# Expert stage of a routed encoder layer: token rows fetched in four column pieces and turned by VectorE

## The chip, the cores and the metric

The kernel runs on one core of one Trainium2 chip. The metric is device time in microseconds (us) of one execution. A core has five instruction queues that matter here: TensorE (PE, matmuls; PEld is its weight load, which overlaps), VectorE (DVE), ScalarE (ACT), GpSimd (POOL) and SyncE (SP). SP issues the plain DMAs, POOL the indirect ones (rows picked by an index) and some small ones. All transfers of a core run on its 16 DMA engines. Data lies in SBUF as 128 partitions; matmul results go to PSUM.

## The reference, cut to what matters

One layer of a streaming encoder over 2048 prompt rows and 128 sample rows of 1024 values, all float32. Token mixing and cross-attention come first and are not touched by the change beyond the places where the expert stage overlaps their end. The expert stage sends every row to 2 of 32 SwiGLU experts:

```
lg = t @ w_rg + b_rg ;  g_idx = argmax(lg) ;  g_w = softmax(lg)[g_idx]
le = (t @ w_re + b_re)[group g_idx] ;  top_v, top_i = top_k(le, 2)
gate = g_w * softmax(top_v) ;  expert = g_idx * 8 + top_i
y = (silu(x @ w_eg[e]) * (x @ w_eu[e])) @ w_ed[e]     # w_eg, w_eu: 1024 x 512, w_ed: 512 x 1024
x = x + sum over the two experts of gate * y ;  out = rms_norm(x) * g_final
```

The experts' sum over the 1024 input values may be taken in any order, as long as the rows of the weights are taken in the same one.

## The kernel before, in words

**Lists.** The attention stage (functions `scores`, `residual`, `logits`, `route`, `place`) ends with each row's two experts. POOL scatters one entry per row and expert into a table in DRAM (`scatter_slots`). One step of the expert stage computes 128 entries: 64 of an expert below 16 (lane 0) and 64 of one from 16 up (lane 1), since PE's output halves can hold two experts side by side. There are steps 0 to 41. Step 0 is computed between the last parts of the attention stage (`gate_early`, `up_early`, `down_early`), steps 1 to 41 by `work`, written out for the first and last ones and looped in between.

**What one step does, engine by engine.**

- POOL, in this order in `work(t)`: `gather_x` fetches the 128 residual rows of step t into `r_x`; `gather(t + 2)` fetches the 128 normalised input rows of step t+2 into `r_x1n`, with the row numbers in `e_token`; `fetch(t + 3)` and `fetch_again(t + 1)` load the lists `e_pair` and `e_spair` in two pieces each; `scatter_x` writes the finished rows back to DRAM; `scatter_out` writes the final output rows. `gather_x(t + 1)` waits for the landing of `scatter_x(t)`, since a row can occur in both. That loop of scatter, landing, gather, landing and addition must close once a step.
- PE, in `work(t)`: gate product (8 k-slices, each two matmuls of 64 stationary columns that run side by side, one for each lane, helper `both`), up product in two halves, `turn_h` of the first half of the hidden rows (2 transposes), `turn_x(t + 1)` (8 transposes of the next step's input rows, L2195, into `r_pst`), `turn_h` of the second half, down product (16 pairs into `r_psx`). Within the down product the order was: k-slices 0 and 1 for both output halves, then 2 and 3.
- ACT: `silu`, then one copy of 256 columns of the turned hidden rows (L1775, needed by the down product's first pairs), then the copy of the first four turned k-slices of the input, `r_pst` to `r_h2T` (L1780), then sums of squares.
- DVE: `tokens(t + 2)` (one cast of the row list, L1957), `rows`, two products of the hidden halves (L1974), the copy of the second half of the turned hidden rows (L1979), the copy of the second four k-slices of the turned input (L1962), two additions of the expert's result (L1993), and the final scaling (L2002).
- SP: loads of the next expert's weights, 2 MB each for gate, up and down, when PE has finished with the buffer (`load_part`, L1286).

Semaphores alone tie the queues; each engine takes its own instructions strictly in order. Several names are reused buffers: `r_x1n` holds the gathered input rows, `r_h2T` their transposes (two buffers each), `r_x1r` holds the SiLU output, the hidden rows and their transposes, and `W` the weights.

**Entry.** Before step 1, PE waits for the rows of step 1: DVE writes the step table, POOL fetches the list (L1584), DVE casts it (L1957), POOL gathers the rows (L1600), PE turns them (L2195), ACT and DVE copy them, and the gate product starts. DVE has the cast for step 2 ahead of its copy for step 1, and that cast waits for step 2's list, which POOL fetches behind step 1's gather.

## Time and profile before

| | us |
|---|---|
| median of 3 runs | 2452.66 (2451.31 to 2457.74) |
| the profiled execution's own time | 2455.3 |
| its span | 2453.6 |
| PE busy | 2385.9 (97%) |
| DVE busy | 1015.2 (41%) |
| ACT busy | 448.8 (18%) |
| POOL busy | 560.1 (23%) |

The span runs from the first to the last recorded instruction; the execution's time is 1.7 us longer. Busy time counts each engine by itself, and a matmul's recorded length (0.59 us for 512 columns) overlaps the next one's, so the distance between starts (0.43 us for a pair) says how fast PE goes. Gate steps of the expert stage follow each other every 22.25 us. In a timeline row the first number is the start, the second the length, and the bracket at the end says how long the engine had been idle and what ended that.

### The profile page before, as it was taken

To read this page: it belongs to the slowest core of one execution; us is meant where nothing else is said; L and a number is where in the kernel's file an instruction comes from. 1 tells how busy PE (TensorE), PEld (TensorE's weight loads), DVE (VectorE), ACT (ScalarE), POOL (GpSimd) and SP (SyncE) were. 2 spreads that over 40 slices of the span, in tenths; PEclk is the share of its full clock that TensorE was granted. 3 is DMA by queue.
4 is the path that set the end of the run, shared out by engine and by line. 5 is a ranking of instruction groups with operands and counts; after the bars stand their busy time and mean duration, and the time that the engine had idled before them with its cause. 6 is when DMAs were issued, how large, how long until landed. Compare 5 with 4: busy or idle time off the path is not lost.

```text
span 2453.6 us, 33018 instructions
## 1 busy us (share of the span) xinstructions
PE 2385.9 (97%) x10639; PEld 1161.2 (47%) x10640; DVE 1015.2 (41%) x2549; ACT 448.8 (18%) x1012; POOL 560.1 (23%) x711
## 2 busy tenths in 40 slices
PE   8999999999999997999999998999999999999998
PEld 4444444444444474444444443444444444444443
DVE  1585665666678112255555543222222222222222
ACT  2222212212211122111111111111111111111111
POOL 1122232132133000011111113232323322323231
PEclk9999999999999999999999999999999999999999
DMA  6202111111132436464444327967497749797994
GB/s 238 108 30 67 39 41 58 39 53 47 40 126 106 149 127 223 148 191 124 122 130 127 117 86 271 340 220 270 169 366 264 261 165 368 262 353 270 350 353 149
DMA packets 186898, 427.31 MB, mean 174 GB/s; under 512 B 27874, under 2 KB 51962, under 8 KB 186666
## 3 DMA queue, kind: packets, MB, share of 16 engines
q1 hardware_dynamic: 155810, 351.41, 42.0%
q0 software_dynamic: 30656, 74.14, 8.3%
q8 instruction: 53, 0.87, 0.1%
q10 hardware_dynamic: 336, 0.54, 0.1%
q14 instruction: 43, 0.35, 0.0%
HBM read 351.89 MB, written 88.52 MB: 179 GB/s over the span
## 4 chain that ended last, share of the span: by engine, by line
PE 57%; DMA 1%; DVE 1%; issue 0%; POOL 0%; ACT 0%; POOLq 0%; SPq 0%; DVEq 0%; ACTq 0%
PE r_pss L2206 17%; PE r_psx L2206 12%; PE r_psx L2165 10%; PE r_pss L2145 9%; PE r_psk L2206 6%; PE r_pst L2195 2%; PE r_psr L2177 1%; PE r_psr L2215 1%; PE r_pss L2215 0%; PE r_pss L2207 0%; DMA table_scratch<-r_val,r_slot 0%; PE r_pss L2251 0%; DMA r_x1n<-h_scratch,e_token 0%; PE r_psx L2207 0%; PE r_psk L2207 0%
## 5 line engine op out<-in xcount | busy, mean ns | idle before, releaser
L790 PE MATMUL a_psz<-W 128*128 128x512 f32 x1088 | 480.0, 594 | 0.1
L2206 PE MATMUL r_pss<-W,r_h2T 128*64 x1312 | 432.3, 488 | 3.3 <-issue 3.3
L2207 PE MATMUL r_pss<-W,r_h2T 128*64 128x256 f32 (+1 forms) x1312 | 432.3, 488 | 0.0
L628 DVE SCALAR_TENSOR_TENSOR yacc<-aext,pcol,yacc 128x256 f32<-128x256 f32 x928 | 370.8, 477 | 0.0
L790 PEld LDWEIGHTS a_psz<-W 128*128 128x128 f32 x1088 | 203.2, 191 | 235.5 <-issue 235.0
L2206 PEld LDWEIGHTS r_pss<-W,r_h2T 128*64 128x64 f32 x1312 | 180.1, 137 | 257.3 <-issue 215.8
L2207 PE MATMUL r_psx<-W,r_x1r 128*64 128x512 f32 x656 | 290.3, 595 | 0.0
L2206 PE MATMUL r_psx<-W,r_x1r 128*64 x656 | 290.3, 595 | 0.0
L2165 PE MATMUL r_psx<-W 128*128 128x512 f32 x544 | 237.6, 594 | 1.2 <-ACT W L1724 1.2
L2145 PE MATMUL r_pss<-W,r_h2T 128*128 128x512 f32 x512 | 225.4, 598 | 2.3 <-PEq L123 2.3
L2207 PEld LDWEIGHTS r_pss<-W,r_h2T 128*64 128x64 f32 x1312 | 180.1, 137 | 0.0
L492 POOL TENSOR_TENSOR W<-W 128x512 f32<-128x512 f32 x34 | 115.6, 3408 | 267.0 <-ACT W L605 267.0
L2206 PEld LDWEIGHTS r_psx<-W,r_x1r 128*64 128x64 f32 x656 | 86.5, 137 | 170.7 <-issue 170.7
L2165 PEld LDWEIGHTS r_psx<-W 128*128 128x128 f32 x544 | 102.1, 190 | 123.8 <-issue 123.8
L2145 PEld LDWEIGHTS r_pss<-W,r_h2T 128*128 128x128 f32 x512 | 96.6, 191 | 118.4 <-issue 118.4
L1993 DVE SCALAR_TENSOR_TENSOR r_x<-r_psx,e_spair,r_x 128x512 f32<-128x512 f32 x84 | 63.0, 751 | 213.6 <-PE r_psx L2207 213.6
L2207 PE MATMUL r_psk<-W,r_h2T 128*64 128x256 f32 x656 | 148.3, 379 | 0.0
L2206 PE MATMUL r_psk<-W,r_h2T 128*64 x656 | 148.3, 379 | 0.0
L957 PE MATMUL a_psz<-W,a_maT 128*128 128x512 f32 x272 | 122.3, 592 | 0.0
L957 PE MATMUL a_psz<-W 128*128 128x512 f32 x272 | 122.3, 592 | 0.0
L1614 POOL DMA_INDIRECT x_scratch<-r_x,e_stoken x41 | 42.7, 1042 | 324.7 <-DVE r_x L1993 304.8
L1974 DVE TENSOR_TENSOR r_x1r<-r_pss,r_x1r 128x256 f32<-128x256 f32 x43 | 18.1, 423 | 229.5 <-PE r_pss L2207 229.5
(358 smaller groups left out, 2618.8 us busy)
## 6 DMA issues: line engine op xcount, KB each, us to landing
W<-in_w_expert_gate SPq DMA_DIRECT2D x32, 2048.0 KB, 12.1
W<-in_w_expert_up SPq DMA_DIRECT2D x32, 2048.0 KB, 11.0
W<-in_w_expert_down SPq DMA_DIRECT2D x32, 2048.0 KB, 10.3
W<-in_x_prompt SPq DMA_DIRECT2D x32, 512.0 KB, 4.2
x_scratch<-W SPq DMA_DIRECT2D x18, 512.0 KB, 3.0
r_x1r<-x_scratch SPq DMA_DIRECT2D x17, 512.0 KB, 4.4
x_scratch<-r_x SPq DMA_DIRECT2D x17, 512.0 KB, 5.2
h_scratch<-r_h SPq DMA_DIRECT2D x17, 512.0 KB, 2.6
```

The source lines that it names most:

```text
L492: pool.tensor_tensor(x, mixed[:, 512 * n:512 * n + 512], x, ALU.add).then_inc(S["x1_half"], 1)
L628: ins = dve.scalar_tensor_tensor(out=out, in0=src, scalar=w, in1=yacc[:, i, :], op0=ALU.mult, op1=ALU.add)
L790: last = pe.matmul(psz[bank][:], hT[t.par][:, k, :], w_in[bank][:, k, :], start=(k == 0), stop=(k == KD - 1))
L957: last = pe.matmul(psz[n][:], (maT[:, k, :] if k < CG else mbl[t.par][:, k - CG, :]), w_out[:, k, 512 * n:512 * n + 512], start=(k == 0), ...
L1614: pool.indirect_dma_start(out=x2_d.rearrange("t p d -> (t p) d"), out_offset=bass.IndirectOffsetOnAxis(ap=stoken[t.par][:], axis=0), in_=y ...
L1993: dve.scalar_tensor_tensor(out=yb[t.par][:, c], in0=psx[:, c], scalar=spair[t.par][:, 1:2], in1=yb[t.par][:, c], op0=ALU.mult, op1=ALU.add ...
L2145: last = pe.matmul(pss[:, 2 * n:2 * n + 2, :].rearrange("p h n -> p (h n)"), h2T[i % 2][:, k, :], A[:, k, 512 * n:512 * n + 512], start=(k ...
L2165: last = pe.matmul(psx[:, 512 * n:512 * n + 512], (pT if i else qT)[:, c, :], (B if i else w_xo)[:, c, 512 * n:512 * n + 512], start=(c == ...
L2177: last = pe.matmul(psr[:, 0:NG + NE], h3T[:, k, :], wr[:, k, :], start=(k == 0), stop=(k == KD - 1))
L2195: last = pe.transpose(pst[:, k, :], xg[t.par][:, P * k:P * k + P], ident[:])
L2206: pe.matmul(out[0:HALF, :], xt[:, 0:HALF], W[:, bass.ds(base + at, n)], start=start, stop=stop)
L2207: return pe.matmul(out[HALF:P, :], xt[:, HALF:P], W[:, at:at + n], start=start, stop=stop)
```

## The change

Five things change in the expert stage.

1. The input rows of a step are no longer turned by PE through `r_pst`. VectorE turns them with one instruction that transposes 32 x 32 blocks (`turn_split`, L222, already used in the attention stage).
2. For that, a gather puts quarter q of the row of token 32b + r into partition 32q + r, columns 256b and up. It is four indirect DMAs of 128 pieces of 1 KB, one for each b, in place of one of 128 rows of 4 KB.
3. The index lists for these are made by VectorE: 16 small operations of 32 x 1 in place of one cast of 128 x 1.
4. The turned rows then have value 8p + k in partition p of slice k. So gate and up weights are loaded with rows `(p k)` in place of `(k p)`: per partition one contiguous run of 16 KB in place of eight of 2 KB. The down weights are as before.
5. The ACT copy of the first half of the turned hidden rows is two copies of 128 columns, and the down product takes slice 0 for both output halves, then slice 1, then 2 and 3. Waits for `x_turned` go; `turn_p` and the gate product have new ones.

```diff
@@ load_part
-                          I[name][0][bass.ds(e, 1), :, :].rearrange("a (k p) n -> p (a k) n", p=P)).then_inc(here, 16)
+                          I[name][0][bass.ds(e, 1), :, :].rearrange("a (k p) n -> p (a k) n" if n == 2 else "a (p k) n -> p (a k) n", p=P)).then_inc(here, 16)
...
@@ POOL, gather(t)
                         pool.wait_ge(T["token_done"], t.v + 1)
-                        need(pool, T["x_turned"], 2 * (t.v - 1))
+                        need(pool, T["xT_done"], t.v - 1)
                         settle(pool)
-                        pool.indirect_dma_start(out=xg[t.par][:], out_offset=None,
-                                                in_=h3_d[0:P * (EARLY + 2), :] if isinstance(t.v, int) and t.v == 0 else h3_d,
-                                                in_offset=bass.IndirectOffsetOnAxis(ap=token[t.par][:], axis=0)).then_inc(x_here[t.par], 16)
+                        h3_rows = h3_d[0:P * (EARLY + 2), :] if isinstance(t.v, int) and t.v == 0 else h3_d
+                        for b in range(QUADS):
+                            c = D // QUADS
+                            pool.indirect_dma_start(out=xg[t.par][:, c * b:c * b + c], out_offset=None,
+                                                    in_=h3_rows.rearrange("t (q c) -> (t q) c", q=QUADS),
+                                                    in_offset=bass.IndirectOffsetOnAxis(ap=token[t.par][:, b:b + 1], axis=0)).then_inc(x_here[t.par], 16)
...
@@ ACT
                     def hT_out(t):
                         act.wait_ge(T["h_turned"], 2 * t.v + 1)
                         act.wait_ge(T["down_done"], t.v + 1)
-                        act.activation(hT[:, 0:2, :], psh[:, 0:2, :], ACT.Copy).then_inc(T["hT_lo"], 1)
-
-                    def xT_out(t):
-                        act.wait_ge(T["x_turned"], 2 * t.v + 1)
-                        need(act, T["up_done"], t.v)
-                        act.activation(xT[t.par][:, 0:4, :], pst[:, 0:4, :], ACT.Copy).then_inc(T["xT_done"], 1)
+                        for k in range(2):
+                            act.activation(hT[:, k, :], psh[:, k, :], ACT.Copy).then_inc(T["hT_lo"], 1)
...
@@ DVE
                     def tokens(t):
                         dve.wait_ge(pair_here[t.par], 32 * (t.half + 1))
-                        need(dve, x_here[t.par], 16 * t.half)
-                        dve.tensor_copy(token[t.par][:], pair[t.par][:, 0:1]).then_inc(T["token_done"], 1)
+                        need(dve, x_here[t.par], 16 * QUADS * t.half)
+                        for b in range(QUADS):
+                            for q in range(QUADS):
+                                last = dve.tensor_scalar(token[t.par][QUAD * q:QUAD * q + QUAD, b:b + 1], pair[t.par][QUAD * b:QUAD * b + QUAD, 0:1],
+                                                         float(QUADS), float(q), ALU.mult, ALU.add)
+                        last.then_inc(T["token_done"], 1)
 
                     def xT_out(t):
-                        dve.wait_ge(T["x_turned"], 2 * t.v + 2)
+                        dve.wait_ge(x_here[t.par], 16 * QUADS * (t.half + 1))
                         need(dve, T["up_done"], t.v)
-                        dve.tensor_copy(xT[t.par][:, 4:8, :], pst[:, 4:8, :]).then_inc(T["xT_done"], 1)
+                        turn_split(dve, xT[t.par][:], xg[t.par][:]).then_inc(T["xT_done"], 1)
...
@@ PE, work(t)
                         turn_h(t, 0)
-                        if j < LAST - 1:
-                            turn_x(t.at(1), (0, 1, 2, 3))
-                            turn_x(t.at(1), (4, 5, 6, 7))
                         turn_h(t, 1)
                         pe.wait_ge(down_here, wanted)
                         need(pe, F["added"], 2 * t.v)
-                        for m in range(2):
-                            pe.wait_ge(T["hT_hi" if m else "hT_lo"], t.v + 1)
+                        for k in range(2):
+                            pe.wait_ge(T["hT_lo"], 2 * t.v + k + 1)
                             for n in range(2):
-                                for k in (2 * m, 2 * m + 1):
-                                    last = both(psx[:, 512 * n:512 * n + 512], hT[:, k, :], base, 8192 + 1024 * k + 512 * n, k == 0, k == KE - 1)
-                                if m:
-                                    last.then_inc(T["down_done" if n else "y_half"], 1)
+                                both(psx[:, 512 * n:512 * n + 512], hT[:, k, :], base, 8192 + 1024 * k + 512 * n, k == 0, False)
+                        pe.wait_ge(T["hT_hi"], t.v + 1)
+                        for n in range(2):
+                            for k in (2, 3):
+                                last = both(psx[:, 512 * n:512 * n + 512], hT[:, k, :], base, 8192 + 1024 * k + 512 * n, False, k == KE - 1)
+                            last.then_inc(T["down_done" if n else "y_half"], 1)
...
@@ PE, between the two halves of the last scores, and before expert_steps
-                            if s + 1 == NT:
-                                pe.wait_ge(S["squares1"], NT - 1)
-                                turn_x(fixed(0), (0, 1, 2, 3))
-                                turn_x(fixed(0), (4, 5, 6, 7))
...
-                    turn_x(fixed(1), (0, 1, 2, 3))
-                    turn_x(fixed(1), (4, 5, 6, 7))
```

The order of instructions on PE at the seam between up and down product of a step, before (`r_psk` is the second half of the up product, `r_psr` and the following `r_pss` are the turned hidden halves, `r_pst` the turned input, `r_psx` the down product):

```order
L2206 MATMUL r_psk<-W,r_h2T 64x256
L2207 MATMUL r_psk<-W,r_h2T 64x256
L2215 MATMUL r_psr<-ident,r_x1r 128x128 x2
L2195 MATMUL r_pst<-ident,r_x1n 128x128 x8
L2215 MATMUL r_pss<-ident,r_x1r 128x128 x2
L2206 ISA
L2206 MATMUL r_psx<-W,r_x1r 64x512
```

And in the changed kernel:

```order
L2192 MATMUL r_psk<-W,r_h2T 64x256
L2193 MATMUL r_psk<-W,r_h2T 64x256
L2201 MATMUL r_psr<-ident,r_x1r 128x128 x2
L2201 MATMUL r_pss<-ident,r_x1r 128x128 x2
L2192 ISA
L2192 MATMUL r_psx<-W,r_x1r 64x512
```

The eight transposes are gone, and the second `turn_h` stands right behind the first.

DVE at the entry, from the cast for step 1 on (`e_token` the row lists, `r_h2T` the turned rows of step 1), before:

```order
L1957 CAST e_token<-e_pair 128x1
L1993 SCALAR_TENSOR_TENSOR r_x<-r_psx,e_spair,r_x 128x512 x2
L2091 CAST p_loads_row<-r_psk 1x96
L1957 CAST e_token<-e_pair 128x1
L1962 COPY r_h2T<-r_pst 128x512
L1999 TENSOR_SCALAR router_w<-router_w 128x1
```

And in the changed kernel:

```order
L1951 TENSOR_SCALAR e_token<-e_pair 32x1 x16
L1989 SCALAR_TENSOR_TENSOR r_x<-r_psx,e_spair,r_x 128x512 x2
L2086 CAST p_loads_row<-r_psk 1x96
L1951 TENSOR_SCALAR e_token<-e_pair 32x1 x16
L222 STREAM_TRANSPOSE r_h2T<-r_x1n 128x4x8x32
L1995 TENSOR_SCALAR router_w<-router_w 128x1
```

Each cast became 16 operations, and the copy of half the slices became the turn of all of them, still behind the list of step 2.

## Rows read from the trace of the kernel before

**Rows 1.** The page, part 1: busy us, share and instructions of each engine.

```profile
PE 2385.9 (97%) x10639; PEld 1161.2 (47%) x10640; DVE 1015.2 (41%) x2549; ACT 448.8 (18%) x1012; POOL 560.1 (23%) x711
```

**Rows 2.** Waits of PE from 1500 us to the end, longest: total, times, longest.

```profile
PE r_pst L2195 <- DMA r_x1n<-h_scratch,e_token: 7.1, 1, 7.1
```

**Rows 3.** Timeline of PE at the seam of a step: start, length, engine, line.

```profile
1718.91 0.38 PE L2207 MATMUL r_psk<-W,r_h2T 128*64 128x256 f32 x1
1719.22 0.44 PE L2215 MATMUL r_psr<-ident,r_x1r 128*128 128x128 f32 x2
1719.50 1.04 PE L2195 MATMUL r_pst<-ident,r_x1n 128*128 128x128 f32 x8
1720.37 0.38 PE L2215 MATMUL r_pss<-ident,r_x1r 128*128 128x128 f32 x2
1720.68 0.64 PE L2206 MATMUL r_psx<-W,r_x1r 128*64 x1
```

**Rows 4.** Timeline of DVE in the same step.

```profile
1710.05 0.14 DVE L1957 CAST e_token<-e_pair 128x1 int32<-128x1 f32 x1
1710.11 0.14 DVE L1985 CAST e_stoken<-e_spair 128x1 int32<-128x1 f32 x1
...
1715.99 0.42 DVE L1974 TENSOR_TENSOR r_x1r<-r_pss,r_x1r 128x256 f32<-128x256 f32 x1 [5.67 <-PE r_pss L2207]
1719.34 0.42 DVE L1974 TENSOR_TENSOR r_x1r<-r_psk,r_x1r 128x256 f32<-128x256 f32 x1 [2.93 <-PE r_psk L2207]
...
1726.17 0.75 DVE L1993 SCALAR_TENSOR_TENSOR r_x<-r_psx,e_spair,r_x 128x512 f32<-128x512 f32 x1 [4.36 <-PE r_psx L2207]
```

**Rows 5.** Timeline of ACT at the seam.

```profile
1719.70 0.39 ACT L1775 ACTIVATE r_x1r<-r_psr 128x256 f32<-128x256 f32 x1 [6.67 <-PE r_psr L2215]
```

**Rows 6.** Groups of DVE by line and form: count, busy us, mean ns.

```profile
L222 DVE STREAM_TRANSPOSE r_h3T<-r_h3s 128x1024 f32<-128x1024 f32 x15 | 30.4, 2030 | 54.1 <-DMA r_h3s<-h_scratch 54.1
```

**Rows 7.** Timeline of POOL, DVE and PE at the entry of step 1.

```profile
1502.76 0.96 POOL L1579 DMA_INDIRECT table_scratch<-r_val,r_slot  x1 [0.30 <-issue]
...
1517.14 1.03 POOL L1600 DMA_INDIRECT r_x1n<-h_scratch,e_token  x1 [5.14 <-issue]
...
1515.82 0.15 DVE L1957 CAST e_token<-e_pair 128x1 int32<-128x1 f32 x1 [6.62 <-DMA e_pair<-table_scratch]
...
1522.48 0.15 DVE L1957 CAST e_token<-e_pair 128x1 int32<-128x1 f32 x1 [5.01 <-DMA e_pair<-table_scratch]
...
1521.95 1.97 PE L2195 MATMUL r_pst<-ident,r_x1n 128*128 128x128 f32 x8 [7.09 <-DMA r_x1n<-h_scratch,e_token]
...
1524.90 1.11 PE L2206 MATMUL r_pss<-W,r_h2T 128*64 x1 [0.98 <-issue]
```

**Rows 8.** Windows: length, busy time by engine, granted clock (PEclk), DMA share, GB/s.

```profile
1524.00:1530.00 6.00, 5.10 (x14) 1.57 (x16) 2.46 (x6) 1.08 (x4) 2.98 (x5) 0.52 0.54 178
```

**Rows 9.** A step beside weight loads: timelines of POOL and DVE.

```profile
2050.79 1.00 POOL L1608 DMA_INDIRECT r_x<-x_scratch,e_stoken  x1 [4.79 <-DMA x_scratch<-r_x,e_stoken]
...
2063.17 1.04 POOL L1614 DMA_INDIRECT x_scratch<-r_x,e_stoken  x1 [6.06 <-DVE r_x L1993]
...
2059.94 0.75 DVE L1993 SCALAR_TENSOR_TENSOR r_x<-r_psx,e_spair,r_x 128x512 f32<-128x512 f32 x1 [4.36 <-PE r_psx L2207]
```

**Rows 10.** DMA issues: issued at 2050.79; then median of 31 scatters, 1600 to 2300.

```profile
r_x<-x_scratch,e_stoken POOLq DMA_INDIRECT x1, 7.9
...
x_scratch<-r_x,e_stoken POOLq DMA_INDIRECT x31, 8.5
```

**Rows 11.** DMA queues, 2058 to 2059 us: packets, MB, share of 16 engines.

```profile
q0 software_dynamic: 65, 0.26, 66.9%
q1 hardware_dynamic: 65, 0.13, 34.5%
```

**Rows 12.** The same from 2062 to 2063 us, weights alone.

```profile
q1 hardware_dynamic: 153, 0.40, 104.5%
```

**Rows 13.** The same from 803 to 810 us, a weight load with rows `(p k)`.

```profile
q1 hardware_dynamic: 80, 2.62, 101.7%
```

More of the change, by code:

```diff
@@ L1369, in build @@
             spair = [sb(f"e_spair{i}", [P, 3]) for i in range(2)]
-            token = [sb(f"e_token{i}", [P, 1], I32) for i in range(2)]
+            token = [sb(f"e_token{i}", [P, QUADS], I32) for i in range(2)]
             stoken = [sb(f"e_stoken{i}", [P, 1], I32) for i in range(2)]
@@ L1687, in work @@
                             for i in range(2):
-                                pool.wait_ge(x_here[i], 16 * (pairs + LAST // 2))
+                                pool.wait_ge(x_here[i], 16 * QUADS * (pairs + LAST // 2))
                                 settle(pool)
@@ L1808, in work @@
                         hT_out(t)
-                        if j < LAST - 1:
-                            xT_out(t.at(1))
-                        else:
-                            act.wait_ge(T["xT_done"], 4 * (pairs + 2))
-                            settle(act)
+                        if j == LAST - 1:
                             act.wait_ge(F["sample_here"], 16)
@@ L2189, in ranks @@
                         pe.matmul(psk[:, 0:NE], ones[:], total[:], start=False, stop=True).then_inc(S["rank_psum"], 1)
-                    def turn_x(t, ks):
-                        if ks[0] == 0:
-                            pe.wait_ge(x_here[t.par], 16 * (t.half + 1))
-                            need(pe, T["xT_done"], 2 * t.v)
-                        for k in ks:
-                            last = pe.transpose(pst[:, k, :], xg[t.par][:, P * k:P * k + P], ident[:])
-                        if ks[-1] in (3, 7):
-                            last.then_inc(T["x_turned"], 1)
                     def weights(t):
@@ L2257, in gate_early @@
                             pe.wait_ge(S["exp_done"], NT - 1)
+                            pe.wait_ge(T["xT_done"], 1)
                         for k in ks:
```

18 lines of the change are left out of this document (7 added, 11 removed).

## The prediction

> **What bounds the kernel now.** I read the page's busy times first, then PE's waits in the expert stage, then one step's timelines, then the entry, then the DMA queues. The reader is to see in the first that PE is the bound: busy for 97% of the span [rows 1]. PE's waits hold one stall of size in the expert stage, 7.1 us, for the gathered rows of step 1 [rows 2]. Between steps there is none: at the seam between up and down product PE goes from its last pair (1718.91) to the turns of the hidden rows (1719.22), the eight input transposes (1719.50), the second turn (1720.37) and the down product (1720.68) without a break [rows 3]. So what leaves PE's queue there is time of the kernel, less what PE then has to wait for. DVE and ACT wait for PE in each step.
>
> **Step by step: the seam.** The transposes take 1720.37 - 1719.50 = 0.87 us per step. They also covered a handover. DVE makes the second half of the hidden rows from 1719.34 to 1719.76 [rows 4], and the second turn needs it. Without the transposes PE is ready for it at 1719.50 and waits until 1719.76 plus a hop of some 0.07 (an estimate; DVE began 0.05 after PE's last recorded end here, 1718.91 + 0.38). It starts at 1719.83, and the down product 0.31 later, the distance of the last two rows in [rows 3]: 1720.14 in place of 1720.68, a gain of 0.54 us. Two things must be there by then. ACT's copy of 256 columns runs from 1719.70 for 0.39 [rows 5]; its new first half, of 128 columns, is shorter, and even at 0.39 it ends at 1720.09. DVE's copy of the other half starts when the second turn is done (about 1720.27) and takes 0.42 (like the L1974 row), so 1720.7; the new order of the down product needs it only after four pairs of 0.43, at 1721.9. The finer order is thus what makes the early start possible. Turns of this kind are issued in steps 1 to 40: 40 x 0.54 = 21.6 us. Bounds: 34.8 if nothing has to be waited for, 12 if the handovers cost 0.24 more each.
>
> **The turn of step 0** stood between two halves of the last scores, where PE has no break: another 0.9 us gone. DVE turns there for 2.03 [rows 6] in place of two copies of 0.65 from PSUM; the softmax behind them is some 0.8 later, which ACT and PE's residual product of the same stage cover.
>
> **DVE in a step.** Its turn takes 2.03 us [rows 6] in place of a copy of 0.68. It stands behind the copy of the hidden half, so from 1720.8 to 1722.8, and the next thing on DVE, the addition, waits for PE until 1726.17 less 0.54 [rows 4]. The turned rows are needed at the next gate product, at about 1727. Nothing. The row list costs 16 operations at a distance of 0.06 to 0.07, as two small casts have (1710.05, 1710.11): 1.0 us more. They fall in DVE's idle stretch of 5.67 us before 1715.99 [rows 4]. Behind them is the cast of `e_stoken`, which the next `gather_x` waits for, but that one waits for POOL's own queue or a landing much longer. Nothing, as long as the stretch is there. ACT loses a copy and gains a short one: nothing.
>
> **POOL in a step.** One gather becomes four. One indirect DMA holds POOL for 1.0 us, and two in a row start 1.26 apart when a wait stands between them (a length of 0.96 and an idle 0.30) [rows 7]; without it nearer 1.05. So 3 x 1.1 = 3.3 us more, 3.1 to 3.8. `scatter_x` is queued behind them, and POOL was idle for 6.06 us before it in a step beside weight loads [rows 9]. 2.7 remain. Nothing, and the cover is thin there.
>
> **The entry.** Here nothing hides the new work. DVE's list for step 1, cast at 1515.82, is 1.0 later. POOL gathers from 1517.14 [rows 7]; now from 1518.2, and 3.3 longer. Its fetch of step 2's list is behind that, so DVE's second cast, at 1522.48 for want of that list, moves by 1.0 + 3.3 to 1526.8, and takes 1.1: 1527.9. Only then does DVE turn step 1's rows, for 2.03: 1529.9. The rows themselves (landed 4.8 after issue at 1517.14, so about 1526 for the last piece) are no longer the last to come; the list of step 2 is. The gate product starts at about 1530.1, was 1524.90: 5.2 later, though the 1.97 of PE's transposes are gone. The clock adds to it. From 1524 to 1530 the granted clock was 0.52 of full, the lower level, after PE had idled for 7.09 us [rows 7, 8]; the slow stretch began before the restart at 1521.95 and ended some 7.6 us after it, and transposes lay in 2.95 us of it. If it lasts as long after a restart at 1530.1, matmuls now take its full loss, 3.8 us in place of 2.3. Entry: +6.7 us; bounds +4 (the gathers at 1.0, a short slow stretch) and +9.
>
> **The sum.** -21.6 - 0.9 + 6.7 = -15.8 us. The profiled execution took 2455.3, so 2439.5; it was 2.6 above the median of the runs shown, 2452.66. Forecast for the median: 2436.9 us, 0.64% less. Own range 2429 to 2445.
>
> **DMA, the unknown.** Bytes are the same. The gather has four times the packets of a quarter the size. The gate and up loads change from 1024 packets of 2 KB to 128 of 16 KB: a load with such rows earlier in this kernel shows 80 packets for 2.62 MB, 33 KB each, so one packet per partition [rows 13]. Their speed is about the same, 0.37 MB/us there and 0.40 at [rows 12]: nothing either way by bytes. What matters is how two queues share the engines. Where gathers and weights overlap, both queues moved 65 packets in one us, one of 4 KB for each of 2 KB [rows 11]: the engines take turns by the packet, whatever its size. The Trainium skill has this as a rule ("DMA: Bandwidth & Descriptors", section "Queues, rings and completion order"): each engine round-robins between its queues and drains a whole packet before it switches. By it the sum would be rival 1's.
>
> Another page speaks against the change altogether: the Trainium skill, "VectorE: DVE Perf Modes", section "Rules for kernel authors", says to transpose 128 x 128 on TensorE if a PSUM destination will do. By that rule the 0.87 would stay. Here the trace has VectorE's slower turn, 2.03 for all eight slices, in an idle stretch, and TensorE's on the path.
>
> **Rival 1, slower: row transfers stuck behind 16 KB packets.** A packet of 16 KB holds an engine for 0.65 us (an estimate: 0.40 MB/us over 16 engines is 25 KB/us each [rows 12]), one of 2 KB for 0.08. A transfer of 128 rows is 8 packets per engine; beside a gate or up load each waits 0.57 longer, 4.6 us in all. The place is the loop scatter, landing, gather, landing, addition. In the step at 2050.79 the gather landed 7.9 later, at 2058.7, and the addition needed it at 2059.94 [rows 9, 10]: 1.25 us spare, and the step is now 0.54 shorter. A late addition does not stop PE at once: DVE has its idle 5.67 less the 1.0 of the lists, so 4.7, before the next hidden rows are late. It decides from the second such step in a row. Scatters landed later than 6 us in 27 of 39 steps (their median is 8.5 [rows 10]), in 8 runs; two free steps in each leave 11, at 4.6 - 1.25 = 3.3 each: +36. 2473 us, and 2460 to 2490 around it. For it: the rows of the two queues. Against: only part of a transfer lies beside gate or up loads, the loads drain in the same time and leave gaps, and most steps have 2 us or more to spare.
>
> **Rival 2, about the same.** The handovers cost more and the entry too: -12 - 0.9 + 9 = -4, or the loop pays in a few steps only: 2449. For it: three engines now pass the baton in 0.9 us of each step. Against: each has an idle bracket in the rows.
>
> **Rival 3, better.** Less waiting at the seam (0.70 a step, between 0.54 and 0.87) and an entry at its low bound: -28 - 0.9 + 4 = -25, 2428; with the upper bound of the seam 2421.
>
> **Rival 4: the turn doesn't leave the path.** If DVE's turn were late for the next gate product, PE would wait there. It has 4 us of room in each step, so this needs rows that land 15 us late. 3%, priced with rival 1.
>
> **How the numbers follow.** Forecast 47%, rival 1 with 4 20%, rival 2 20%, rival 3 13%. Under 0.3% (7.4 us, 2445.3 to 2460.0) a measurement of this kernel can't be told from no change. Faster: 45 of the forecast's 47, rival 3's 13, 5 of rival 2: 63%. Same: 2, 14 and 2 of rival 1: 18%. Slower: 18 and 1: 19%. The range reaches from rival 3, 2424, into rival 1, 2466; below lie about 5%, above 13%.
>
> **What would show it.** Right: no PE transposes from `r_x1n`; steps 21.7 us apart; a wait of about 0.3 us before the second `turn_h` and none before the down product; the turn on DVE followed by a wait for PE; a PE wait of some 15 us before step 1, ended by DVE. Rival 1: the additions wait for a DMA, steps longer than 22 us in the stretches with weight loads, none elsewhere. Wrong: PE waits before the gate product in each step, or the down product waits for ACT.

## The result and the profile after

| | before | changed |
|---|---|---|
| median of 4 runs, us | 2451.98 (2450.96 to 2457.74) | 2480.78 (2479.83 to 2482.87) |
| span of the profiled execution | 2453.6 | 2478.2 |
| mean granted clock | 0.993 | 0.986 |
| PE busy | 2385.9 | 2369.8 |

The ratio is 1.0114, with a 95% interval of 1.0096 to 1.0131: slower by 1.1%, where 0.64% faster was forecast and 2424 to 2466 was the range.

PE's waits from 1550 us on, after the entry, in the profile of the changed kernel (engine, what waited, what ended it: us in total, times, longest):

```profile
PE r_pss L2201 <- DVE r_x1r L1970: 18.6, 29, 2.9
PE r_pss L2201 <- ACT r_x1r L1779: 13.4, 6, 3.2
PE r_pss L2192 <- issue: 2.3, 1, 2.3
PE r_psx L2192 <- ACT r_x1r L1779: 1.1, 1, 1.1
```

L2201 are the turns of the hidden rows, where there was next to no stall before (0.2 us in all). The forecast allowed for a handover of about 0.3 us in each step; 2.9 and 3.2 are something else. Not every step has it. From one step's first addition to the next's there are 40 distances: many are 21.79 or 21.87 us (22.25 before), others about 23.4, and the longest 27.6. The steps that are not disturbed are thus 0.42 us shorter, and the disturbed ones take back more than all steps could give: from the first addition of step 1 to that of the last step it is 910.74 us, and it was 892.12.

Here is a disturbed seam, PE first (start, length, engine, line, operation, and in brackets the idle time before it with what ended it), then DVE, ACT and POOL:

```profile
1751.54 0.38 PE L2192 MATMUL r_psk<-W,r_h2T 128*64 x1
1751.55 0.38 PE L2193 MATMUL r_psk<-W,r_h2T 128*64 128x256 f32 x1
1751.86 0.44 PE L2201 MATMUL r_psr<-ident,r_x1r 128*128 128x128 f32 x2
1754.06 0.44 PE L2201 MATMUL r_pss<-ident,r_x1r 128*128 128x128 f32 x2 [1.76 <-DVE r_x1r L1970]
...
1748.59 0.42 DVE L1970 TENSOR_TENSOR r_x1r<-r_pss,r_x1r 128x256 f32<-128x256 f32 x1 [3.14 <-PE r_pss L2193]
1753.58 0.42 DVE L1970 TENSOR_TENSOR r_x1r<-r_psk,r_x1r 128x256 f32<-128x256 f32 x1 [4.57 <-remote]
...
1753.70 0.45 ACT L1779 ACTIVATE r_x1r<-r_psr 128x128 f32<-128x128 f32 x2 [7.96 <-PE r_psr L2201]
...
1747.59 0.97 POOL L1603 DMA_INDIRECT r_x1n<-h_scratch,e_token  x1 [0.31 <-issue]
1748.87 0.95 POOL L1603 DMA_INDIRECT r_x1n<-h_scratch,e_token  x1 [0.30 <-issue]
1750.12 0.94 POOL L1603 DMA_INDIRECT r_x1n<-h_scratch,e_token  x1 [0.30 <-issue]
1751.37 0.94 POOL L1603 DMA_INDIRECT r_x1n<-h_scratch,e_token  x1 [0.30 <-issue]
1752.30 1.18 POOL L1584 DMA_DIRECT2D e_pair<-table_scratch  x2
```

PE's last matmul of the up product ends at 1751.93 by the records and its first turn at 1752.30. DVE waits for the one, ACT for the other, and both start only at 1753.58 and 1753.70. The semaphore updates of these two PE instructions stand in the trace at 1753.56 and 1753.60, so 1.63 and 1.30 us after the ends, 0.04 apart, as if both had been held and let go together. In an undisturbed step DVE starts 0.04 after the end. The recorded ends of matmuls are modelled, so they alone don't exclude that PE itself stood still; that the two updates come 0.04 apart, where the two ends are 0.37 apart, speaks for held updates. "remote" is how the profile names a release that it can't match with an instruction: the update came too late for it. What stands beside the gap on another engine is POOL, which issues the four gathers and then the list fetches.

Where POOL stands tells which steps are hit. In 14 steps of this trace the first list fetch begins between 0.37 and 1.82 us after the end of the up product, so that at least three of the four gathers have begun by then: in all 14 the update is 1.5 us late or more. In the steps where the fetch begins later than 3 us after it, the update is on time (0.03 us at most).

The waits of DVE count these cases:

```profile
DVE r_x1r L1970 <- PE r_psk L2193: 75.2, 26, 3.2
DVE r_x1r L1970 <- remote: 68.0, 14, 6.0
...
DVE r_x L1989 <- DMA r_x<-x_scratch,e_stoken: 36.6, 8, 6.5
```

14 second products of the hidden rows were late, each after 4.9 us of idle time on average where the others have some 2.9: 14 x 1.96 = 27 us. (The expectations below say 15 steps; in the fifteenth the up product's update is late by 0.3 only, that of the turn by 1.3.) Behind the longest stalls PE then runs at its lower clock: 0.50 of full speed from 1778 to 1784 in the windows below (window, length, busy times and counts of PE, PEld, DVE, ACT, POOL, granted clock, DMA share, GB/s).

```profile
1776.00:1778.00 2.00, 0.00 (x0) 0.00 (x0) 0.00 (x0) 0.00 (x0) 1.83 (x3) 0.93 0.99 400
1778.00:1780.00 2.00, 1.14 (x4) 0.59 (x6) 0.84 (x3) 0.45 (x2) 1.33 (x3) 0.50 1.04 284
1780.00:1782.00 2.00, 2.00 (x6) 0.46 (x4) 1.95 (x2) 0.00 (x0) 0.00 (x0) 0.50 0.73 279
```

One more thing is odd in this trace: it lacks semaphore records. It has 14,341 updates that come from DMAs, and a later trace of the same program (e5) has 16,148.

The entry came out close to the forecast. DVE, POOL and PE there:

```profile
1515.31 2.52 DVE L1951 TENSOR_SCALAR e_token<-e_pair 32x1 int32<-32x1 f32 x16 [4.67 <-DMA e_pair<-table_scratch]
...
1525.90 2.52 DVE L1951 TENSOR_SCALAR e_token<-e_pair 32x1 int32<-32x1 f32 x16 [6.48 <-DMA e_pair<-table_scratch]
1528.45 2.01 DVE L222 STREAM_TRANSPOSE r_h2T<-r_x1n 128x1024 f32<-128x1024 f32 x1
...
1518.67 1.02 POOL L1603 DMA_INDIRECT r_x1n<-h_scratch,e_token  x1 [4.58 <-DVE e_token L1951]
...
1522.53 0.94 POOL L1603 DMA_INDIRECT r_x1n<-h_scratch,e_token  x1 [0.30 <-issue]
...
1530.66 1.11 PE L2192 MATMUL r_pss<-W,r_h2T 128*64 x1 [13.12 <-issue]
```

The gate product of step 1 starts at 1530.66; 1530.1 was forecast, 1524.90 it was before [rows 7].

### The profile page after: what moved, and what is told of

Same layout as the page of the kernel before. It is cut to its first block, busy times and chain, and to the rows that moved or that the text cites. A ratio compares the mean times of both kernels' runs of the same rounds, so it can differ in the third digit from the quotient of the medians.

```text
span 2478.2 us, 33004 instructions
## 1 busy us (share of the span) xinstructions
PE 2369.8 (96%) x10303; PEld 1134.2 (46%) x10304; DVE 1165.6 (47%) x3178; ACT 426.9 (17%) x1012; POOL 681.2 (27%) x837
## 4 chain that ended last, share of the span: by engine, by line
PE 55%; another core or an unknown queue 2%; DVE 1%; issue 1%; DMA 0%; ACT 0%; POOL 0%; SPq 0%; DVEq 0%; ACTq 0%; POOLq 0%
PE r_pss L2192 16%; PE r_psx L2192 12%; PE r_psx L2160 10%; PE r_pss L2140 8%; PE r_psk L2192 4%; PE r_psr L2172 1%; PE r_pss L2201 1%; DVE r_x1r L1970 1%; PE r_pss L2193 0%; PE r_pss L2236 0%; PE r_psr L2201 0%; PE r_psx L2274 0%; PE r_psx L2193 0%; PE r_psk L2193 0%
## 5 line engine op out<-in xcount | busy, mean ns | idle before, releaser
L2192 PE MATMUL r_psx<-W,r_x1r 128*64 x656 | 297.6, 607 | 2.1 <-ACT r_x1r L1779 1.1
L2193 PE MATMUL r_psx<-W,r_x1r 128*64 128x512 f32 x656 | 297.7, 608 | 0.0
L1603 POOL DMA_INDIRECT r_x1n<-h_scratch,e_token x168 | 161.2, 960 | 66.8 <-issue 59.9
L222 DVE STREAM_TRANSPOSE r_h2T<-r_x1n 128x1024 f32<-128x1024 f32 x58 | 117.7, 2029 | 5.4 <-DMA r_gffn<-in_g_ffn 5.4
```

What stands on the lines that cost most here:

```text
L222: return dve.transpose(dst.rearrange("p k (b r) -> p b k r", r=QUAD), src.rearrange("p (b a k) -> p b k a", b=QUADS, a=QUAD))
L1603: pool.indirect_dma_start(out=xg[t.par][:, c * b:c * b + c], out_offset=None, in_=h3_rows.rearrange("t (q c) -> (t q) c", q=QUADS), in_off ...
L2192: pe.matmul(out[0:HALF, :], xt[:, 0:HALF], W[:, bass.ds(base + at, n)], start=start, stop=stop)
L2193: return pe.matmul(out[HALF:P, :], xt[:, HALF:P], W[:, at:at + n], start=start, stop=stop)
```

## The experiments

**First round: which part of the change.** Four kernels on one chip. The theory H was that the four gathers hold back PE's signals; the rival W was rival 1 of the prediction, the 16 KB packets.

`e1_one_gather`, waits adapted:

```diff
-  for b in range(QUADS): pool.indirect_dma_start(out=xg[t.par][:, c * b:c * b + c], ...)
+  pool.indirect_dma_start(out=xg[t.par][:], out_offset=None, in_=h3_rows, in_offset=...token[t.par][:, 0:1]...)
...
-  float(QUADS), float(q), ALU.mult, ALU.add)
+  1.0, 0.0 * q, ALU.mult, ALU.add)
```

> The changed kernel with one gather of whole rows (4 KB) per step instead of four of quarter rows; the 16 list operations stay, but write the plain row number, so the turned rows are not the right ones. Theory H (held signals): in 15 of the 40 loop steps of the changed kernel the semaphore updates of PE (end of the up product, end of the first turn) reach DVE and ACT 1.3 to 3.1 us after the matmul's recorded end, while GpSimd issues the four gathers and then the list fetches; DVE's second hidden product is late by as much, 27 us in all. With one gather no update is late, the steps are 21.8 us, and the entry is some 4 us shorter: 2480.8 - 27 - 7 (low-clock stretches behind these stalls) - 4 = about 2443 us. Rival W (16 KB weight packets hold up the row transfers and the rest): the weights still come in such packets, so only the entry's 4 us go: about 2476.

`e2_rows_2k`:

```diff
-  rearrange("a (k p) n -> p (a k) n" if n == 2 else "a (p k) n -> p (a k) n", p=P)
+  rearrange("a (k p) n -> p (a k) n", p=P)
```

> The changed kernel with the gate and up weights loaded as before the change, in rows of 2 KB (the order of the contraction then doesn't fit the turned rows, so the products are others). H: the late updates stay in as many steps; only additions that wait for their rows get earlier, at most 7 us: 2474 to 2481. W: the excess over 21.8 us per step goes (37 us in all): 2450 or less.

`e3_before_4_gathers`, on the kernel before:

```diff
-  pool.indirect_dma_start(out=xg[t.par][:], ..., token[t.par][:] ...)
+  for b in range(QUADS): pool.indirect_dma_start(out=xg[t.par][:, c * b:c * b + c], ..., token[t.par][:, b:b + 1] ...)
-  dve.tensor_copy(token[t.par][:], pair[t.par][:, 0:1])
+  for b in range(QUADS): last = dve.tensor_scalar(token[t.par][:, b:b + 1], pair[t.par][:, 0:1], float(QUADS), float(b), ALU.mult, ALU.add)
```

> The kernel before with its gather cut in four (quarter rows of the same 128 tokens, a list of four columns), everything else as before; it computes the reference. H: PE's updates come 1.3 us or more late in some 10 to 15 of the steps here too; the first turn has eight transposes (0.87 us) between it and the second, which cover part, so +0.7 us or more for each, and the entry grows by some 4: 2462 to 2475. W: no late updates, only the entry: 2456 to 2458.

`e4_gather_first`, GpSimd's order in the loop:

```diff
-  gather_x(t)
   if j < LAST - 2:
       gather(t.at(2))
+  gather_x(t)
```

> The changed kernel with one move: in the loop GpSimd issues the four gathers (for the step after next) ahead of the gather of the residual rows instead of behind it, so they start when the row list is ready, some 6.7 us before the end of the up product, and end 1.7 before it. It computes the reference. H, if only gathers in progress hold the updates: the steps with a late update go, about 2450. H, if the whole string of issues does it: as many or more late updates, 2475 to 2500. W: the packets are the same, 2475 to 2485.

| | median, us | ratio to before | interval |
|---|---|---|---|
| before | 2454.86 | | |
| e1, one gather | 2443.3 | 0.9945 | 0.9928 to 0.9961 |
| e2, 2 KB rows | 2445.56 | 0.9955 | 0.9939 to 0.9972 |
| e3, before + 4 gathers | 2455.35 | 1.0005 | 0.9995 to 1.0014 |
| e4, gathers first | 2447.55 | 0.9967 | 0.9955 to 0.998 |

No PE update is late in any of the four. Taken alone, e1 spoke for H and e2, against its expectation, for W, while in e3 the four gathers cost nothing. That contradicts both theories, unless the changed kernel itself would not have been slow here, and it did not run in this round. e1 and e2 don't compute the layer's result (the rows and the weights no longer fit each other).

**Second round: the changed kernel again, the packets, the entry.** On another chip than the first. `e5_changed_again` has no edit.

> The changed kernel once more, not edited. If the late updates belong to this program (four gathers and 16 KB packets together, since without either there were none), they come back in the same steps: 2475 to 2485, 12 or more of the 40 steps with a PE update over 1.2 us late. If they belong to one loading of the program, this one has other steps or none: down to 2447.

`e6_interleaved` puts an expert's gate slice k at column 1024 k of `W` and its up slice k at 1024 k + 512, so that a contiguous run is 2 KB and partition p still holds rows 8p + k:

```diff
-  eng.dma_start(dst.rearrange("p (k n) -> p k n", k=k),
+  eng.dma_start(dst.rearrange("p (k n) -> p k n", k=k) if n == 2 else dst.rearrange("p (k g n) -> p g k n", g=2, k=k)[:, n, :, :],
...
-  last = both(psg, xT[t.par][:, k, :], base, 512 * k, ...)
+  last = both(psg, xT[t.par][:, k, :], base, 1024 * k, ...)
```

(the up product likewise, and the first gate load of the stage is issued at s == 2, when the columns are free).

> The changed kernel with the gate and up weights of an expert interleaved in W (gate slice k at 1024 k, up slice k at 1024 k + 512), so that each contiguous run is 2 KB again while partition p still holds rows 8p + k. It computes the reference. Both theories of the packets' length (W: they hold up rows; H2: together with the four gathers they delay PE's updates): as e2, 2443 to 2448 us, no late update, no addition that waits for its rows. If it was the order of the weight rows in memory (16 KB contiguous per partition in DRAM) and not the packet: about 2480 still.

`e7_entry_order`, e6 with this:

```diff
   fetch(fixed(1))
-  gather(fixed(1))
   fetch(fixed(2))
+  gather(fixed(1))
...
-  tokens(fixed(2))
   dve.wait_ge(S["s_psum"], NT - 1)
   xT_out(fixed(1))
+  tokens(fixed(2))
```

> e6 with the entry reordered: GpSimd fetches the list of step 2 ahead of the gathers of step 1, and DVE turns step 1's rows before it makes the list of step 2. PE's wait before step 1 was 15.6 us in e2, ended by DVE's turn behind the 16 list operations (2.5 us), which waited for a fetch behind the gathers. By the entry theory the turn comes 2 to 4 us earlier: 2440 to 2444. If the rows land last, nothing: as e6.

`e8_before_16k`, on the kernel before:

```diff
-  rearrange("a (k p) n -> p (a k) n", p=P)
+  rearrange("a (k p) n -> p (a k) n" if n == 2 else "a (p k) n -> p (a k) n", p=P)
```

> The kernel before with the gate and up weights alone loaded in 16 KB runs (products of other rows than the reference's). W, rival 1 of the prediction at its full price: +25 to +36, 2478 to 2490. Late updates need the four gathers as well: none here; a few additions wait for their rows as in e1 (6 waits there), +2 to +6: 2455 to 2461.

| | median, us | ratio to before | interval |
|---|---|---|---|
| before | 2454.79 | | |
| e5, the changed kernel | 2443.73 | 0.9957 | 0.994 to 0.9973 |
| e6, interleaved | 2443.53 | 0.9957 | 0.994 to 0.9974 |
| e7, entry order | 2441.85 | 0.9948 | 0.9932 to 0.9965 |
| e8, before + 16 KB | 2453.29 | 0.9997 | 0.9987 to 1.0007 |

The same program that took 2480.78 us took 2443.73 here: 0.4% faster than before, not 1.1% slower. No update is late. This is what the profile of e5 has for PE's waits in the same stretch as above:

```profile
PE r_pss L2201 <- DVE r_x1r L1970: 5.3, 35, 0.2
PE r_pss L2192 <- issue: 2.3, 1, 2.3
```

The instructions stand where they stood: in 15 steps the first list fetch begins 0.37 to 1.94 us after the end of the up product, as in the hit steps of the first trace, and all updates are on time. Here the end is at 1743.79, with three gathers before it and the fourth in progress:

```profile
1743.83 0.42 DVE L1970 TENSOR_TENSOR r_x1r<-r_psk,r_x1r 128x256 f32<-128x256 f32 x1 [2.96 <-PE r_psk L2193]
...
1743.23 0.95 POOL L1603 DMA_INDIRECT r_x1n<-h_scratch,e_token  x1 [0.30 <-issue]
1744.18 1.17 POOL L1584 DMA_DIRECT2D e_pair<-table_scratch  x2
```

So the delay goes with a position beside POOL's string, but that position alone doesn't make it. The loop is 33.4 us longer in the first trace than in e5 (910.74 and 877.37): PE's waits at the seam are 34.2 against 5.3, which is 28.9 of it; the rest fits the stretches at the lower clock behind them (an estimate, as the remainder).

Rival 1 gets its own measurement in e8 (which also doesn't compute the layer's result). The row transfers are late as it said:

```profile
DVE r_x L1993 <- DMA r_x<-x_scratch,e_stoken: 34.0, 6, 6.4
```

There is no such wait in the kernel before. But the distances of the first additions are then 24.27 and 20.23, or 23.79 and 20.71: the addition is late once, PE never waits, and the next is back in time. From the first addition of step 1 to that of the last step it is 892.15 us, as before (892.12). Only a second late transfer in a row would have cost something, as the prediction had it, and there was none. e7 brings PE to step 1 2.1 us earlier (a wait of 11.8 in place of 13.9), within what it expected; in the medians this does not stand out.

**Third round: is it the chip, and how good can the entry be.** On a third chip. `e9_changed_third` has no edit.

> The changed kernel unedited, for the third time. In the first (2480.8 us) PE's updates were late in 15 loop steps and 11% of the trace's DMA semaphore records were missing; in the second (2443.7) none was late and none missing. If late updates are the rare case of one loading of the program: 2441 to 2446 us, no late update. If every other loading or chip has them: about 2480.

`e10_entry_by_pe` is e6 with step 1 alone prepared as before the change:

```diff
-  gather(fixed(1))
+  pool.indirect_dma_start(out=xg[1][:], out_offset=None, in_=h3_d, ...token[1][:, 0:1]...).then_inc(x_here[1], 16)
...
+  for k in range(KD):
+      last = pe.transpose(pst[:, k, :], xg[1][:].rearrange("p (a k) -> p k a", k=KD)[:, k, :], ident[:])
...
-  tokens(fixed(2))
   dve.wait_ge(S["s_psum"], NT - 1)
-  xT_out(fixed(1))
+  dve.wait_ge(T["x_turned"], 2)
+  dve.tensor_copy(xT[1][:, 4:8, :], pst[:, 4:8, :]).then_inc(T["xT_done"], 1)
+  tokens(fixed(2))
```

> The interleaved version (e6) with step 1 alone prepared as before the change: one gather of whole rows, a list made by one cast, eight transposes on PE (with a stride of 8 columns, since partition p must hold rows 8p + k) and copies by ACT and DVE; DVE makes the list of step 2 behind that. Entry theory: of the +5.6 us that the entry costs in the changed kernel, the three further gathers (3.8), the list operations (2.5) and the list of step 2 leave the path; the first addition of step 1 comes at 1546 to 1549 us in place of 1553, so 2436 to 2440 us. Rival: PE's transposes with a stride are slow or step 2's list is late instead: as e7, 2442.

`e11_old_down_order`, on e6:

```diff
-  for k in range(2): act.activation(hT[:, k, :], psh[:, k, :], ACT.Copy).then_inc(T["hT_lo"], 1)
+  act.activation(hT[:, 0:2, :], psh[:, 0:2, :], ACT.Copy).then_inc(T["hT_lo"], 2)
```

(and the down product in the order of the kernel before)

> e6 with part 5 of the change undone: one ACT copy of 256 columns and the down product in its old order of slices. By the prediction's numbers ACT's longer copy (0.39) still ends 0.05 us or more before PE can start, and DVE's half is needed after four pairs in either order: same as e6, 2443.5 +- 2, steps of 21.83. If the finer order is what makes the early start possible, as the prediction's sentence has it: the down product starts up to 0.1 us later in 39 steps, up to +4.

| | median, us | ratio to before | interval |
|---|---|---|---|
| before | 2455.19 | | |
| e9, the changed kernel | 2485.5 | 1.0121 | 1.0102 to 1.0139 |
| e10, entry by PE | 2480.5 | 1.0106 | 1.009 to 1.0123 |
| e11, old down order | 2499.19 | 1.0182 | 1.0165 to 1.0199 |

The slow times are back on this chip, and for every kernel with the four gathers, 2 KB runs or not: PE's updates are late, and semaphore records are missing again (14,423 from DMAs in e9). The kernel before is not slow here. So the 16 KB packets are not the condition, and the chip is part of it. The expectation of e10 (2436 to 2440) could not be tested here either. That of e11 was wrong on the finer order: its undisturbed steps are 21.95 and 22.03 us, with the change's order 21.79 and 21.87. PE and ACT in e11, and then in e5:

```profile
1728.66 0.44 PE L2202 MATMUL r_psr<-ident,r_x1r 128*128 128x128 f32 x2
1729.25 0.44 PE L2202 MATMUL r_pss<-ident,r_x1r 128*128 128x128 f32 x2 [0.16 <-DVE r_x1r L1971]
1729.82 0.64 PE L2193 MATMUL r_psx<-W,r_x1r 128*64 x1
...
1729.19 0.38 ACT L1780 ACTIVATE r_x1r<-r_psr 128x256 f32<-128x256 f32 x1 [6.64 <-PE r_psr L2202]
```

```profile
1700.03 0.44 PE L2201 MATMUL r_psr<-ident,r_x1r 128*128 128x128 f32 x2
1700.62 0.44 PE L2201 MATMUL r_pss<-ident,r_x1r 128*128 128x128 f32 x2 [0.15 <-DVE r_x1r L1970]
1701.14 0.64 PE L2192 MATMUL r_psx<-W,r_x1r 128*64 x1
...
1700.59 0.45 ACT L1779 ACTIVATE r_x1r<-r_psr 128x128 f32<-128x128 f32 x2 [6.67 <-PE r_psr L2201]
```

In undisturbed steps the down product starts 1.16 or 1.24 us after the first turn with one copy of 256 columns, and 1.00 or 1.08 with two of 128 (the step of e5 that is shown is the one with 1.11): 0.16 apart, as the steps are. ACT's first copy is shorter by 0.1 (0.28 us for one of the two, 0.38 for the one of 256), and there is a quarter of a microsecond between ACT's end (1729.57) and PE's next start (1729.82) that the prediction left out.

**Fourth round: what the slow chips need.** The changed kernel ran beside the others as a mark of the chip (`m_changed_fourth`). `e13` is e1 and `e14` is e3, not edited. `e12_hybrid_gather_first` is e10 with e4's order.

> The changed kernel unedited, as the mark of the chip it runs on: either about 2480 to 2486 with late updates of PE in 12 or more loop steps and missing records, or 2441 to 2446 with none.

> The hybrid (e10: 2 KB runs, step 1 prepared by PE) with the four gathers issued ahead of the gather of the residual rows, so that they end 1.7 us before the up product does. If the late updates come from gathers in progress when PE signals: none or a few even on a chip that shows them, 2438 to 2446 on either. If the string of issues does it wherever it stands: on such a chip as e10, 2480 or more.

> The changed kernel with one gather of whole rows per step and plain row numbers in the list (the turned rows are not the right ones), as e1. On a chip where m_changed has late updates: none here if the four gathers are their condition, 2438 to 2446. If anything else of the change is: about 2476.

> The kernel before with its gather cut in four, as e3 (2455.35 against 2454.86 there). On a chip where m_changed has late updates: if the four gathers alone are the condition, late updates here too, partly covered by PE's eight transposes between the two turns of the hidden rows, +10 to +25: 2465 to 2480. If something of the changed seam is needed: 2455.

| | median, us | ratio to before | PE updates late by 1 us or more in the loop |
|---|---|---|---|
| before | 2454.3 | | |
| changed kernel | 2485.53 | 1.0125 (1.0096 to 1.0155) | 30 |
| e12, gathers first | 2491.01 | 1.0139 (1.0114 to 1.0163) | 63 |
| e13, one gather | 2443.83 | 0.9952 (0.9936 to 0.9968) | 0 |
| e14, before + 4 gathers | 2492.01 (one run) | 1.015, no interval | 78 |

The mark says that this chip is one of the slow ones, and then the others decide. With one gather the rest of the change is 0.5% faster than before, though e13, like e1, doesn't compute the layer's result. The kernel before with four gathers instead of one, and nothing else, takes 2492.01 us (span 2488.9); the same file took 2455.35 in the first round. That is more than its expectation had (2465 to 2480), and it is one run: a second one took 9553.66 us; I have no explanation for that run and leave it out. e14's DVE rows:

```profile
1608.91 0.42 DVE L1979 TENSOR_TENSOR r_x1r<-r_psk,r_x1r 128x256 f32<-128x256 f32 x1 [2.96 <-PE r_psk L2212]
1613.26 0.42 DVE L1984 COPY r_x1r<-r_pss 128x256 f32<-128x256 f32 x1 [3.92 <-remote]
```

And PE's waits in e13, from 1550 us on:

```profile
PE r_pss L2198 <- DVE r_x1r L1967: 8.8, 37, 0.6
PE r_pss L2189 <- issue: 2.3, 1, 2.3
```

In e13 22 updates are late too, one by 0.8 us and the others by 0.6 at most, and its trace has 13,824 updates from DMAs where that of e1, the same program, has 14,137: one gather makes the delay small, it doesn't end it. In e12 the four gathers begin 5.9 us before the end of the up product in place of 4.3, most steps are about 23.2 us, and the gathers first are no cure: the update is let go about 1.25 us after the first list fetch begins, in both orders. That was the second reading of e12's expectation. Whether it is the four issues that count or their 512 pieces of 1 KB in place of 128 of 4 KB, no run separates.

**Fifth round: the gathers in a quiet stretch.** `e15_quiet_gathers` is e10, `e16_changed_quiet_gathers` the changed kernel, with this order on GpSimd:

```diff
   gather_x(t)
-  if j < LAST - 2:
-      gather(t.at(2))
   if j < LAST - 3:
       fetch(t.at(3))
   if j < LAST - 1:
       fetch_again(t.at(1))
+  if j < LAST - 2:
+      pool.wait_ge(T["h_turned"], 2 * t.v + 2)
+      gather(t.at(2))
```

> The hybrid (2 KB runs, step 1 prepared by PE, gathers in the place of the change), unedited. On a chip that shows late updates 2477 to 2490 as before; on one that shows none the entry's 3 to 6 us come out of e6's time: 2436 to 2440.

> The hybrid with the list fetches ahead of the gathers and the gathers held back until both turns of the hidden rows are done (0.9 us after the up product). They then run for 5 us beside the down product, end 3.5 us before the scatter, and their rows are needed a step later. Theory (a late update costs only where an engine waits for it): the same on either kind of chip, 2436 to 2444, PE's waits at the second turn back to 5 or 6 us in all. Rival (the four gathers delay whatever signal comes, so now that of the down product's halves, for which the additions, the scatter and in the end the next gather wait): 2455 or more on a chip with late updates.

> The changed kernel with this one edit of GpSimd's order (fetches first, gathers behind both turns of the hidden rows), 16 KB runs and entry as in the change. Same theory: 2441 to 2447 on either kind of chip; rival: 2460 or more on one with late updates.

| | median, us | ratio to before | interval |
|---|---|---|---|
| before | 2455.24 | | |
| e10 again | 2435.94 | 0.9921 | 0.9904 to 0.9937 |
| e15, quiet gathers | 2434.97 | 0.9915 | 0.9898 to 0.9931 |
| e16, changed kernel + quiet gathers | 2444.11 | 0.9954 | 0.9938 to 0.9971 |

By e10 this chip has no late updates, so what e15 and e16 were made for was not tested: whether the quiet place helps on a chip that has them stays open. What is shown is that it costs nothing there, and that e10 and e15 are 0.8% faster than the kernel before and 0.3 to 0.4% faster than e16, the changed kernel with the quiet place; the changed kernel itself did not run on this chip. Both are 0.1 to 1.0 us below their ranges. The step's gathers now start behind the second turn and end 1.3 to 3.1 us before the scatter:

```profile
1736.77 1.01 POOL L1605 DMA_INDIRECT r_x1n<-h_scratch,e_token  x1 [1.89 <-PE r_pss L2214]
1738.09 0.97 POOL L1605 DMA_INDIRECT r_x1n<-h_scratch,e_token  x1 [0.30 <-issue]
1739.37 0.95 POOL L1605 DMA_INDIRECT r_x1n<-h_scratch,e_token  x1 [0.30 <-issue]
1740.62 0.95 POOL L1605 DMA_INDIRECT r_x1n<-h_scratch,e_token  x1 [0.30 <-issue]
1744.68 1.00 POOL L1619 DMA_INDIRECT x_scratch<-r_x,e_stoken  x1 [3.11 <-DVE r_x L2000]
```

The entry in e10, where PE's transposes with a stride of 8 columns take the 1.97 us that those of the kernel before took [rows 7]:

```profile
1521.25 1.97 PE L2345 MATMUL r_pst<-ident,r_x1n 128*128 128x128 f32 x8 [6.23 <-DMA r_x1n<-h_scratch,e_token]
...
1524.39 1.11 PE L2203 MATMUL r_pss<-W,r_h2T 128*64 x1 [1.17 <-DVE r_h2T L2099]
```

The gate product of step 1 starts at 1524.39, 6.3 us before that of the changed kernel.

## Why the prediction was wrong

The step that failed is "POOL in a step", with its sentence "2.7 remain. Nothing, and the cover is thin there." The three further gathers were weighed as time on POOL's queue, and as such they did cost nothing: the scatter is not late. But in the run of the result, and on two of the five chips used later, the string of four gathers and the list fetches goes with PE signals that arrive up to 3.1 us late, and the seam between up and down product, where three engines hand over in 0.9 us, lies just there. e13 and e14 show on one chip that the four gathers are what it takes there: with one, 2443.83; with four in the kernel before, 2492.01 (one run). Why the updates are held, and why on some chips only, stays open. No rival had this. Rival 1 gave a time near the result (2473) by a mechanism that the runs refute: its transfers are late, in e8, at no cost, and e6 and e10 without them are no faster and no slower for it.

From e5, the same program where no update is late, the other steps can be judged. It took 2443.73, ratio 0.9957, so about -10.6 us in place of -15.8; its span is 9.2 us shorter.

- The seam: 0.42 per step in place of 0.54 (22.25 - 21.83), in 39 steps: -16.4. The handover to DVE was right (0.15 of wait, the second turn 0.59 after the first; 0.61 forecast). The down product was forecast 0.31 behind the second turn [rows 3] and starts 0.41 to 0.52 behind it: PE waits for ACT's first copy and the quarter of a microsecond between them, which the forecast put at nothing. The term is mis-sized by 0.12, within its bounds. That "the finer order is what makes the early start possible" holds (e11: 0.16 a step), though by the numbers beside it in the forecast, a copy of 0.39 that ends in time, it would not have been needed.
- In all the loop takes 877.37 us, 14.8 less than before. The 1.7 that are missing to 16.4 lie in one step near the end, that of PE's 2.3 us wait (which the profile puts to no engine): it takes 24.39 in e6 and 26.09 in e2 and e7, whose loops are 875.6, 877.3 and 877.3. The difference is the clock: behind the same wait e2, e5 and e7 have a stretch at the lower level, of 3.4 us at half speed, and e6 and the kernel before have none (e7, restart at 2340.29, then e6, restart at 2342.72; windows as above):

```profile
2340.00:2345.00 5.00, 4.71 (x14) 1.53 (x16) 1.28 (x1) 0.00 (x0) 2.31 (x3) 0.66 1.02 409
...
2343.00:2348.00 5.00, 5.00 (x26) 1.71 (x24) 1.47 (x3) 0.00 (x0) 1.74 (x3) 1.00 1.03 414
```

- The entry: the gate product at 1530.76, forecast 1530.1; the first addition of step 1 is 5.6 later than before, with the turn of step 0 (-0.9) and the entry (+6.7) together +5.8. The number is near, in part by luck. e5's trace runs 1.0 later than that of before already at 1106 us, where nothing of the change acts yet; counted from there it is 4.6. In it are 1.7 us that no term had, another such stretch, at 1468 us, which neither the trace of before nor that of the changed kernel in the fourth round has (e5, then before, windows as above):

```profile
1467.00:1472.00 5.00, 4.29 (x6) 1.89 (x7) 3.33 (x15) 1.13 (x4) 0.39 (x1) 0.66 0.14 53
...
1467.00:1472.00 5.00, 4.53 (x11) 2.17 (x12) 3.11 (x13) 0.90 (x4) 0.16 (x1) 1.00 0.13 52
```

- The turn of step 0 gave its 0.9: between two additions about it there are 29.70 us in e5, and 30.58 before.
- The lists of the entry: a list takes 2.52 us and not 1.0, since the 16 operations are 0.157 apart, where two casts of other tiles were 0.06 apart [rows 4]; but the second list begins at 1525.90 in place of 1526.8, so the turn starts at 1528.45 where 1527.9 was forecast.
- DVE's turn off the path: right. It takes 2.03, then DVE waits 3.0 us for PE.
- The clock: right in kind, too large in size. It fell during PE's idle stretch (13.9 us in e5) and was at 0.50 until 5.2 us after the restart, where the forecast had 7.6 us, taken over from before. So the matmuls lost about 2.6 us (half of 5.2) and not 3.8, next to nothing more than the 2.3 before.

The prediction's signs of right and wrong served well: they said that "a wait of about 0.3 us before the second `turn_h`" belongs to it (0.15 in e5, with the turn's start 0.59 after the first's as against 0.61), and what the first trace had there, 1.76 and 2.9, belonged to none of the rivals.

## What to carry to other kernels

Run the same program a second time on another chip before you explain a difference of 1%: here the same file is 1.2% slower than before on some chips and 0.4% faster on others, each within about 0.4% of itself. When engines idle with nothing to wait for, compare the time of the semaphore's update with the end of the instruction that makes it. And weigh a string of DMA issues on GpSimd not only as time on its own queue but by which handovers of other engines lie beside it; one gather is the safer form. A quiet place for the four cost nothing where no update is late, and was not tried where they are.

## What was not expected of the hardware

- PE's updates were held 1.2 to 3.1 us and came out 0.04 us apart, 0.9 to 1.3 us after the start of the first list fetch behind four indirect DMAs, on three occasions of the changed kernel (29 to 30 late by 1 us or more in the loop), and never in e5. In e14 some were held up to 4.0 us.
- In each trace with late updates records of semaphores are missing (14,341, 14,423 and 14,318 from DMAs of 16,148 in those three). All timed executions here were traced. The Trainium skill, "NOTIFIC — the notification-queue block", section "Overflow: three behaviours, one of which stalls the engine", says that this block's internal pipeline presses back on the producers rather than lose a record. If that path were congested, late updates would fit; that records are lost here as well does not fit this sentence of the page. No run shows the cause, and whether the updates are late without a trace is open.
- Weights in 16 KB runs made six transfers of rows late in e8, for waits of 34.0 us on DVE, and cost PE nothing.
- An operation on 32 x 1 elements into another group of partitions takes a slot of 0.157 us on DVE, a cast of 128 x 1 one of 0.07.
